# Sample attention: rows numbered by query, dilation and head; values weighed in four column quarters

## What is computed

```python
def _dilated_attn_sample(q, k, v, k_buf, v_buf):
    b, t, h, dh = q.shape                       # 8, 4, 8, 64
    n_buf = k_buf.shape[1]                      # 2048
    k_all = jnp.concatenate([k_buf.astype(k.dtype), k], axis=1)
    v_all = jnp.concatenate([v_buf.astype(v.dtype), v], axis=1)
    outs, lses = [], []
    for window, dilation in DILATED_CONFIGS:    # (128,1), (512,4), (2048,16)
        n_keys = window // dilation + 1
        idx = n_buf + jnp.arange(t)[:, None] - dilation * jnp.arange(n_keys)[None, :]
        ...
        kg, vg = k_all[:, idx], v_all[:, idx]
        sc = jnp.einsum('bthd,btjhd->bthj', q, kg).astype(jnp.float32) * dh ** -0.5
        ...
        lse = jax.nn.logsumexp(sc, axis=-1)
        p = jnp.exp(sc - lse[..., None])
        outs.append(jnp.einsum('bthj,btjhd->bthd', p.astype(v.dtype), vg))
        lses.append(lse)
    return _merge_dilations(outs, lses).astype(q.dtype)
```

## Time and profile before

| | |
|---|---|
| runs shown | 3364.83, 3377.41, 3398.41 us |
| median | 3377.41 us |
| span of the profiled execution | 3370.7 us |
| instructions | 74753 |
| TensorE busy | 3109.9 us (92%) |
| VectorE busy | 1313.1 us (39%) |
| ScalarE busy | 998.6 us (30%) |
| GpSimd busy | 332.7 us (10%) |
| mean granted TensorE clock | 0.969 |

### The profile page before, as it was taken

The page is one execution under the profiler, slowest core; times in us unless marked ns, Lnnn a source line. Parts: engine busy times, 40 slices in busy tenths (PEclk is TensorE's granted clock), DMA queues, the critical chain, the costliest instruction groups (busy, mean ns, idle before and its releaser), DMA issues. The chain is left out here.

```text
span 3370.7 us, 74753 instructions
## 1 busy us (share of the span) xinstructions
PE 3109.9 (92%) x30909; PEld 2115.1 (63%) x30910; DVE 1313.1 (39%) x3231; ACT 998.6 (30%) x2127; POOL 332.7 (10%) x358
## 2 busy tenths in 40 slices
PE   5999999999989989988999979996999999999990
PEld 4677666776668888887766745554555555555540
DVE  3454345544344334436655456664111111111117
ACT  3345323542222222236544543331111111111112
POOL 0000000000010000113333100000100110010004
PEclk9999999999989999999999989997999999999995
DMA  6111112111233333227656474415777776676658
GB/s 213 64 69 55 56 47 72 66 48 41 76 142 116 141 115 128 91 75 223 202 174 173 129 239 151 153 56 203 244 263 268 268 271 217 244 274 244 219 193 313
DMA packets 284899, 533.88 MB, mean 158 GB/s; under 512 B 94642, under 2 KB 108850, under 8 KB 278500
## 3 DMA queue, kind: packets, MB, share of 16 engines
q1 hardware_dynamic: 238732, 390.77, 33.8%
q10 hardware_dynamic: 25128, 66.26, 6.1%
q0 software_dynamic: 20784, 73.15, 5.9%
HBM read 395.40 MB, written 134.72 MB: 157 GB/s over the span
## 5 line engine op out<-in xcount | busy, mean ns | idle before, releaser
L287 PE MATMUL proj_main_ps<-proj_xt,proj_w 128*128 128x257 f32 x1536 | 349.6, 380 | 0.0
L287 PEld LDWEIGHTS proj_main_ps<-proj_xt,proj_w 128*128 128x128 f32 x1536 | 288.9, 190 | 40.7
L2694 PE MATMUL moe_y_ps<-moe_w,moe_ht 128*64 128x512 f32 x1312 | 301.3, 601 | 3.2 <-ACT moe_ht L2733 3.2
L2451 PE MATMUL out_proj_ps<-out_w,out_ct 128*128 128x512 f32 x544 | 241.8, 598 | 5.5 <-DMA out_w<-in_w_out_dram 5.5
L352 PE MATMUL proj_main_ps<-proj_w,proj_xt 128*128 128x512 f32 x512 | 225.3, 593 | 0.0
L2744 ACT ACTIVATE moe_sg<-moe_gate 128x256 f32<-128x256 f32 x82 | 31.4, 383 | 540.1 <-PE moe_gate L2678 540.1
L2694 PEld LDWEIGHTS moe_y_ps<-moe_w,moe_ht 128*64 128x64 f32 x1312 | 87.3, 137 | 158.8 <-issue 155.4
L2780 DVE COPY moe_y<-moe_y_ps 128x512 f32<-128x512 f32 x82 | 56.7, 691 | 313.9 <-PE moe_y_ps L2694 313.9
L2451 PEld LDWEIGHTS out_proj_ps<-out_w,out_ct 128*128 128x128 f32 x544 | 101.8, 192 | 121.3 <-issue 120.5
L1316 DVE COPY_PREDICATED rwkv_t<-ahead_rwkv_cons,rwkv_level_ps 128x512 f32<-128x512 uint32 (+1 forms) x168 | 109.8, 664 | 171.1 <-PE rwkv_level_ps L1031 171.1
L352 PEld LDWEIGHTS proj_main_ps<-proj_w,proj_xt 128*128 128x128 f32 x512 | 97.1, 190 | 108.5 <-issue 107.1
(11 more groups left out here) (403 smaller groups left out, 5476.3 us busy)
## 6 DMA issues: line engine op xcount, KB each, us to landing
moe_w<-in_expert_w_dram SPq DMA_DIRECT2D x64, 2048.0 KB, 9.4
y_rows<-rwkv_zero POOLq DMA_DIRECT2D x65, 512.0 KB, 5.0
kept_first_gate<-in_expert_w_dram SPq DMA_DIRECT2D x16, 2048.0 KB, 9.5
kept_first_up<-in_expert_w_dram SPq DMA_DIRECT2D x16, 2048.0 KB, 15.1
y_rows<-moe_y ACTq DMA_DIRECT2D x164, 128.0 KB, 6.0
ft_p<-proj_uf SPq DMA_DIRECT2D x32, 642.0 KB, 3.2
rwkv_feat<-ft_p SPq DMA_DIRECT2D x12, 1284.0 KB, 6.8
att_s_k<-in_cache_att_k_dram ACTq DMA_DIRECT2D x14, 1024.0 KB, 6.9
```

What stands on the lines that cost most here:

```text
L287: last = mm(out[:, 0:w + 1], W[:, k, kind * C + m * P:kind * C + (m + 1) * P], XT[n % 2][:, k, 0:w + 1], start=(k == 0), stop=(k == KT - 1))
L2451: last = mm(proj_ps[j][:], CT[t % 2][:, k, :], W[:, k, 512 * j:512 * (j + 1)], start=(k == 0), stop=(k == KT - 1))
L2694: last = mm(py[j * HB:(j + 1) * HB, :], HT[:, c, r * HB:(r + 1) * HB], W2[s][:, k, j * 512:(j + 1) * 512], start=(k == 0), stop=(k == FE / ...
```

## The change

1. Rows are numbered by query, dilation, head, with room for a fourth dilation that is never used: SG = 4 x 8 = 32 rows for each query, NQ = 4 x 32 = 128. The masks, the score sums, the transposes, the exponentials and `own_heads` work on 128 rows in place of 96.
2. `weigh_sample` writes the four queries' rows to four ranges of 32 partitions of the bank: for each dilation and query one product with a stationary operand of 32 columns, and one for each query on the new rows, 12 + 4 in place of 9 + 1. The values are the moving operand, 512 columns, as before.
3. `by_tile`, `PB` and the constant `tile_of` go. VectorE's copy in `copy_probs` puts the 96 used columns straight to their places in `LM`, of which the rest is zero; GpSimd's memsets for that (of `SS`, `SNM` and `LM`) stand ahead of `ones_set`. TensorE waits for `s_probs` in place of `s_lm`.
4. The keys of the new rows are kept in `OM` in place of `LM`; `mask_new` becomes three instructions; `sum_new` also waits for `ones_set`.
5. `o_s` and `m_s` are laid out by token, dilation (four), head; a sample is stored with two transfers in place of six, and `output_projection` reads the first three dilations.

```diff
-NQ = 3 * T * H
+SG = 4 * H
+NQ = T * SG
...
-        LM = sb("s_lm", [P, NT, NQ])
-        KNA = LM[:].rearrange("p i q -> p (i q)")[0:B * T, 0:C]
+        LM = sb("s_lm", [P, 3 * (NQ + H)])
+        own_columns = LM[:].rearrange("p (c x) -> p c x", c=3)[:, :, 0:NQ].rearrange("p c (t y) -> p c t y", t=T)[:, :, :, 0:H]
+        by_config = lambda x: x.rearrange("p (t c h) -> p c t h", t=T, c=4)[:, 0:3]
...
-        PB, PN = sb("s_pb", [P, NQ]), sb("s_pn", [T, NQ])
+        PN = sb("s_pn", [T, NQ])
...
+        KNA = OM[0:B * T, :]
...
-                for c in range(3):
-                    rows = slice(c * T * H, (c + 1) * T * H)
-                    sp.dma_start(os_out[c, b * T:(b + 1) * T, :].rearrange("t (h k) -> (t h) k", h=H), OS[b % 2][rows, :]).then_inc(s_st[b % 2], 16)
-                    sp.dma_start(ms_out[c, b * T:(b + 1) * T, :].rearrange("t (h o) -> (t h) o", o=1), ML[b % 2][rows, 1:2]).then_inc(s_st[b % 2], 16)
+                sp.dma_start(os_out[b * T:(b + 1) * T].rearrange("t c (h k) -> (t c h) k", h=H), OS[b % 2][:]).then_inc(s_st[b % 2], 16)
+                sp.dma_start(ms_out[b * T:(b + 1) * T].rearrange("t c (h o) -> (t c h) o", o=1), ML[b % 2][:, 1:2]).then_inc(s_st[b % 2], 16)
...
         def _(g):
+            for x in (SS, SNM, LM):
+                nc.gpsimd.memset(x[:], 0.0)
...
-            def by_tile(b):
-                g_.wait_ge(s_probs, b + 1)
-                if b >= 1:
-                    g_.wait_ge(s_weighted, b)
-                else:
-                    g_.wait_ge(s_new, 1)
-                nc.gpsimd.tensor_tensor(LM[:], PB[:].rearrange("p (o q) -> p o q", o=1).broadcast_to([P, NT, NQ]), tile_of, ALU.mult).then_inc(s_lm, 1)
-
...
             for b in range(B):
                 for j in range(3):
                     product(b, j)
-                if b >= 1:
-                    by_tile(b - 1)
-            by_tile(B - 1)
...
             def weigh_sample(b):
                 pe.wait_ge(sv_ld, 64 * b + 64)
-                pe.wait_ge(s_lm, b + 1)
-                for i in range(NT):
-                    mm(t_ps[1][0:NQ, :], LM[:, i, :], SV[:, i, :], start=(i == 0), stop=False, skip_group_check=True)
-                mm(t_ps[1][0:NQ, :], PN[:], VN[:], start=False, stop=True, skip_group_check=True).then_inc(s_weighted, 1)
+                pe.wait_ge(s_probs, b + 1)
+                for c in range(3):
+                    for t in range(T):
+                        mm(t_ps[1][t * SG:(t + 1) * SG, :], LM[:, c * NQ + t * SG:c * NQ + (t + 1) * SG], SV[:, 1 + (c - 1) * T + t if c else 0, :],
+                           start=(c == 0), stop=False, skip_group_check=True)
+                for t in range(T):
+                    last = mm(t_ps[1][t * SG:(t + 1) * SG, :], PN[:, t * SG:(t + 1) * SG], VN[:], start=False, stop=True, skip_group_check=True)
+                last.then_inc(s_weighted, 1)
...
             def sum_new():
+                v.wait_ge(ones_set, 1)
                 v.wait_ge(s_new, 1)
...
-                v.scalar_tensor_tensor(SNM[:].rearrange("p (c q) -> p c q", c=3), SN[:].rearrange("p (o q) -> p o q", o=1).broadcast_to([B * T, 3, T * H]),
-                                       DH ** -0.5, new_mask.rearrange("p (c q) -> p c q", c=3), ALU.mult, ALU.add).then_inc(s_new_masked, 1)
+                for c in range(3):
+                    last = v.scalar_tensor_tensor(by_config(SNM[:])[:, c], SN[:].rearrange("p (t h) -> p t h", t=T), DH ** -0.5, by_config(new_mask)[:, c], ALU.mult, ALU.add)
+                last.then_inc(s_new_masked, 1)
...
-                v.tensor_reduce(SS[:, 32 * g:32 * g + 32], PRD[(3 * b + g) % 2].rearrange("p t (h k) -> p (t h) k", h=H), AX.X, ALU.add).then_inc(s_sum, 1)
+                v.tensor_reduce(by_config(SS[:])[:, g], PRD[(3 * b + g) % 2].rearrange("p t (h k) -> p t h k", h=H), AX.X, ALU.add).then_inc(s_sum, 1)
...
-                v.tensor_copy(PB[:], t_ps[1][:, 0:NQ])
+                v.tensor_copy(own_columns, by_config(t_ps[1][:, 0:NQ]))
                 v.tensor_copy(PN[:], t_ps[1][0:T, NQ:2 * NQ]).then_inc(s_probs, 1)
...
-    o_s, m_s = scratch("o_s", 3, TS, H * VW), scratch("m_s", 3, TS, H)
+    o_s, m_s = scratch("o_s", TS, 4, H * VW), scratch("m_s", TS, 4, H)
```

More of the change, by code:

```diff
@@ L1424, in attention @@
         weighted, o_copied = sem("weighted"), sem("o_copied")
-        MS = sb("s_masks", [P, 2 * NQ + NT * NQ + C])
+        MS = sb("s_masks", [P, 2 * NQ + C])
         buf_mask, new_mask = MS[:, 0:NQ], MS[0:B * T, NQ:2 * NQ]
-        tile_of = MS[:, 2 * NQ:(2 + NT) * NQ].rearrange("p (i q) -> p i q", i=NT)
-        diag = MS[0:NQ, (2 + NT) * NQ:]
+        diag = MS[:, 2 * NQ:]
         SQ = ring("s_q", [P, T, C], 2)
@@ L1441, in attention @@
         s_prod, s_sum, s_masked, s_turned, s_scores = sem("s_products"), sem("s_sums"), sem("s_masked"), sem("s_turned"), sem("s_scores_copied")
-        s_max, s_neg, s_exp, s_back, s_probs, s_lm = sem("s_max"), sem("s_negated"), sem("s_exps"), sem("s_turned_back"), sem("s_probs_copied"), sem("s_by_tile")
+        s_max, s_neg, s_exp, s_back, s_probs = sem("s_max"), sem("s_negated"), sem("s_exps"), sem("s_turned_back"), sem("s_probs_copied")
         s_weighted, s_own, s_o, s_st = sem("s_weighted"), sem("s_own_head"), sem("s_o_ready"), [sem(f"s_stored{j}") for j in range(2)]
@@ L1529, in _ @@
             for j in range(2):
-                sp.wait_ge(s_st[j], 96 * (B // 2))
+                sp.wait_ge(s_st[j], 32 * (B // 2))
         @blk.gpsimd
         def _(g):
+            for x in (SS, SNM, LM):
+                nc.gpsimd.memset(x[:], 0.0)
             for j in range(NV):
@@ L1564, in _ @@
             nc.gpsimd.tensor_tensor(PRD[1][0:B * T], wide(KNA, B * T), PRD[0][0:B * T], ALU.mult).then_inc(s_new, 1)
-            g.wait_ge(s_in, 16)
             for b in range(B):
@@ L1762, in sample_exp @@
                 if b >= 2:
-                    a.wait_ge(s_st[b % 2], 96 * (b // 2))
+                    a.wait_ge(s_st[b % 2], 32 * (b // 2))
                 nc.scalar.activation(PR[:], SX[:], ACT.Exp, bias=ML[b % 2][:, 1:2], accum_out=OS[b % 2][:, DH:VW]).then_inc(s_exp, 1)
@@ L1835, in maxima @@
                 if b >= 2:
-                    v.wait_ge(s_st[b % 2], 96 * (b // 2))
+                    v.wait_ge(s_st[b % 2], 32 * (b // 2))
                 v.tensor_copy(SX[:, P:P + T], SNT[:, b * T:(b + 1) * T])
@@ L1890, in sample_masks @@
 def sample_masks():
-    c, t, h = np.meshgrid(np.arange(3), np.arange(T), np.arange(H), indexing="ij")
-    c, t, h = c.reshape(-1), t.reshape(-1), h.reshape(-1)
+    t, c, h = np.meshgrid(np.arange(T), np.arange(4), np.arange(H), indexing="ij")
+    t, c, h = t.reshape(-1), c.reshape(-1), h.reshape(-1)
     i = np.arange(P)[:, None]
@@ L1896, in sample_masks @@
     j = i % T
-    new = np.where(np.where(c[None] > 0, j == t[None], j <= t[None]), 0.0, NEG)
-    tile = np.where(c == 0, 0, T * (c - 1) + 1 + t)
-    sel = np.broadcast_to((np.arange(NT)[:, None] == tile[None]).reshape(1, -1), (P, NT * NQ))
-    diag = np.zeros((P, H, DH))
-    diag[:NQ] = (np.arange(H)[None] == h[:, None])[:, :, None]
-    return np.ascontiguousarray(np.concatenate([buf, new, sel, diag.reshape(P, -1)], 1).astype(np.float32))
+    new = np.where(np.where(c[None] > 0, j == t[None], j <= t[None]) | (c[None] == 3), 0.0, NEG)
+    diag = np.repeat(np.arange(H)[None] == h[:, None], DH, 1)
+    return np.ascontiguousarray(np.concatenate([buf, new, diag], 1).astype(np.float32))
 G = 4
@@ L2955, in hybrid_layer @@
         groups = [dict(y=yr_p, gates=gt_p, o=o_p, m=m_p, x=a["x_prompt"], rows=P, tiles=TP, seq=None, first=0, out=y_p),
-                  dict(y=yr_s, gates=gt_s, o=o_s, m=m_s, x=a["x_sample"].rearrange("b j d -> (b j) d"), rows=TS, tiles=1, seq=SJ, first=S, out=y_s)]
+                  dict(y=yr_s, gates=gt_s, o=o_s[:, 0:3].rearrange("t c k -> c t k"), m=m_s[:, 0:3].rearrange("t c k -> c t k"), x=a["x_sample"].rearrange("b j d -> (b j) d"), rows=TS, tiles=1, seq=SJ, first=S, out=y_s)]
         output_projection(nc, groups, a["w_out"], a["norm_ffn_g"],
```

## The result

The changed kernel takes 3340.19 us (median of 4 runs, 3338.22 to 3342.23) where the kernel before takes 3376.76 in the same comparison (4 runs, 3364.83 to 3398.41): ratio 0.9873, interval 0.9836 to 0.9911. The two medians are 36.6 us apart, 1.08%; the ratio, 1.27%, is the comparison's own and not their quotient. The interval excludes 1, so the kernel is faster, but by less than the comparison's bound of 2%, under which its class is "same"; the prediction had taken that bound as 1%. The profiled execution has a span of 3338.5 us, 32.2 less than the 3370.7 of before.

The account below looks back on a forecast made before the run. TensorE's time was taken to bound the attention stage. Eight samples save 39.5 us, less 0.5 charged once, so 39 us off the 3377.4 us median gives 3338 us; range 3324 to 3370.

Parts of the forecast that it names:

- What bounds it: Attention stage, samples' stretch: time is TensorE's time, busy 237.38 of 240 us; only what TensorE sheds or gains counts.
- Full abreast: Samples' value products: four quarters run at once, 8 slots, 3.48 us; 3.93 with extras against 8.87 per sample; chance 0.58.
- the reading limit (3366): Rival: reading carries only two streams, so two passes abreast, gain 12 us, 3366; chance 0.25 with the program-order road.
- three changes of the array's shape: Value block: switches into quarters, to the 4-row form and out cost 0.35 us a sample, bounds 0.17 and 0.45.
- Loads: Attention stage: cached values' and keys' loads still land in time at the quicker pace; none comes in late.
- Wider transposes: Transposes back and the scores' transpose, 128 instead of 96 columns: 0.1 us a sample in all, bounds 0 and 0.1.
- `by_tile`, the wider rows, the copies: GpSimd's 16.3 us step removed, 128 rows and larger copies: worth nothing; new-row copy at worst 2.4 us in all.
- Memsets: Three memsets ahead of ones_set delay SyncE's queue by up to 0.9 us, once; likely hidden, 0.9 us if not.
- mask_new: VectorE, once: one instruction becomes three, from 2 us less to 5.8 more; 0.5 charged to the end, bounds 0 and 6.
- the last product 39 us earlier: Sign that the forecast is right: the last attention product comes 39 us earlier.
- the gain is taken back: Rival: a late key load or a VectorE stall eats half the gain, leaving 20 us, 3357; chance 0.08.
- a bound of 1% between faster and same: Class limit assumed at 1%, 34 us; chances faster 0.48, same 0.44, slower 0.08.

Follow-up runs that it names:

- e5: Changed kernel with the twelve cached-row products computed twice (48 passes instead of 24), same result; 3363.79 us, ratio 0.9959 to the kernel before.
- e2: Changed kernel with only the column quarters undone (nine products of 128 columns, one for new rows; no by_tile); 3381.65 us, ratio 1.0023 to before.
- e7: Changed kernel with the three memsets behind ones_set instead of ahead of it; 3337.7 us, ratio 0.9892 to the kernel before.
- e4: Changed kernel with its products ordered by pairs of quarters: queries 0 and 1 in turn, then 2 and 3; 3341.99 us, ratio 0.989 to before.
- e1: The changed kernel timed once more, no edit; 3348.82 us, ratio 0.9905 to the kernel before.
- e11: The changed kernel once more, no edit, beside e9 and e10; 3346.16 us, ratio 0.9908 to the kernel before.
- e9: Changed kernel with one 128-column product per dilation, three of four queries' value tiles of dilations 4 and 16 left out; 3337.38 us, ratio 0.9882 to before.
- e6: Changed kernel with every sample two units later (first_at 15 instead of 13); 3341.07 us, ratio 0.9902 to the kernel before.
- e10: Changed kernel with samples two units later and the memsets behind ones_set, together; 3334.56 us, ratio 0.9867 to the kernel before.
- e12: The kernel of e10 timed and profiled once more; 3334.78 us, ratio 0.987 to the kernel before.
- e3: Changed kernel with the query as outer loop, so six passes in a row go to one quarter; 3361.8 us, ratio 0.9951 to before.

## Why the prediction was right

The forecast was 3338 us; the kernel takes 3340.19, faster by 1.08% by the medians and 1.27% by the comparison's ratio. That it came so near is in part luck: the 16 executions of the changed kernel in three comparisons have a median of 3345.2.

*What bounds it:* right. The stretch is TensorE's time; its idle time in a period, 0.48 us, did not grow.

*Full abreast:* right. Starts by fours, 6 slots for 24 passes, durations of a pass unchanged: a partition that feeds four streams costs nothing, and the reading limit (3366) falls. The block was 3.70, not 3.93. With 8 slots of 0.435, 3.48, three changes of the array's shape are left with 0.22 us, not 0.35; e5's extra 24 passes cost 2.58, 0.43 a slot, which confirms the slot. I had taken the price of a change between the two bounds; it was nearer the lower one. The error is 0.13 us a sample, and 0.1 more since the wider transposes, which I had added to the block, lie outside of it.

*Loads:* as forecast, none reaches the path. GpSimd's wait for queries is 47.3 us now, and no wait of TensorE follows from it. *Wider transposes:* 0.1 us a sample forecast; 5.17 of the block less 5.02 of the whole period leaves 0.15. Right to 0.4 us in all.

*`by_tile`, the wider rows, the copies:* worth nothing as forecast; e2, which keeps them and undoes the quarters, is the kernel before in time. *Memsets:* hidden, e7. They are 0.20, 0.20 and 0.43 us long, and load_v(0) was issued 0.75 us after the stage's first product where it was 0.09 before. *mask_new:* three instructions of 172, 173 and 2822 ns, 3.17 us in place of the 2.89 of the earlier trace rows, so 0.3 us on VectorE and not the 0.5 charged to the end; of the 6 us bound nothing came. The view by line of the changed kernel:

```profile
L1809 DVE SCALAR_TENSOR_TENSOR att_s_snm<-att_s_sn,att_s_masks x3: 172/173/2822, 1561.4 to 1564.3; 32x32 f32<-32x32 f32 x3
```

*The gain reaches the end:* the step that was off. The profile shed 5.02 x 8 = 40.2 us at full clock and got back 8, so "the last product 39 us earlier" was 32, counted from the stage's start. I had given "the gain is taken back" 0.08 and looked for it in VectorE and a late key load. It came through TensorE's clock, which stood at full level in all of this stretch in the profile of before, so no row showed a fall there. Of those 8 us, the 2.85 at the stage's start need not be the change's: e2, without the quarters, has the same 17.07 us at low clock there, and e4 and e5, with them, have the 6.83 of before. The size varies by execution: against the first profile, e1 and e11 lost 9 and 14 us more. The median still came out near the forecast since that size is inside the spread between comparisons: the medians are 36.6 us apart in the first comparison, 28.7 in e1's (3377.49 to 3348.82) and 33.2 in e11's (3379.33 to 3346.16). The forecast's 39 is the number for a full clock. The chances were worked out with a bound of 1% between faster and same, 0.48 and 0.44; with the comparison's bound of 2% a gain of 39 us is "same" from the outset.

What stays open is what lets the clock fall. The profiles show falls in the samples' stretch with a shortened block only (none in before, twice, nor in e2; the spread of before's clock over its executions allows no stronger word). They show one without narrow passes (e9), some with a longer dense block (e5), and that where they lie goes with the samples' place in the pipeline (e6, e10, e12). In the first profile of the changed kernel each fall of the samples' stretch begins 8 to 9 us ahead of a block, behind a light unit with the transposes back and a wait of 0.48 us; e1's at 1813.8 and e11's at 1826.55 do not. The same wait stands at the same place in four periods of before, without a fall.

## What to carry to other kernels

Products with few stationary columns that share their moving length can be put into column quarters of the array and run four abreast in f32 at no loss per pass; cost them by slots and add little for the changes of shape (0.22 us for three here). Write them so that consecutive products go to different quarters. When the last percent counts, read the granted clock of the stretch that was shortened, in more than one profile, and that of every execution, since a profile is one of them: the time saved at full clock is not the time that the end gets.

## What the runs showed of the hardware

- The same 24 passes take 2.71, 3.60 and 5.36 us in three orders. All three come out if each column quarter takes in two f32 products and a third one for it holds back all behind it.
- Four column quarters over all 128 rows run with passes of 596 ns, as one full-width product's 595, and one start of four per 0.43 us.
- TensorE's granted clock was 0.50 through 30.65 us in which it was busy 30.65 (e1), and through 58.62 of 58.62 us in e3, the part within 1960 us of the longest stretch on record, 68.27 us. A stretch of 3.41 us cost the changed kernel about 1.5 us.
- The scores of dilation 4, whose columns are read with a stride, take 2.20 us at the low clock (e5) and 2.19 at the full one, while the transposes behind them go from 1.10 to 1.97.

The windows of e3:

```profile
1901.38:1960.00 58.62, 58.62 (x311) 53.24 (x310) 21.05 (x140) 29.83 (x94) 0.00 (x0) 0.50 0.26 70
```
